# A recurrent turn in which the second gate product, the second convolution's taps and the low parts stand elsewhere

## The chip, the cores and the metric

One core of a Trainium2 chip runs the whole program in one launch. The metric is the device time of an execution in microseconds (us). Of an execution the profiler gives the span, from the first to the last instruction. Five engines matter: PE (matrix products), DVE (VectorE), ACT (ScalarE), POOL (GpSimd) and SP, which here only issues transfers. Each engine works its own list of instructions in order; semaphores order them between engines.

## The reference, cut to what matters

A two-layer encoder on 1040 positions of width 1024. The first layer is a bidirectional gated recurrence of width 2048, and the change lies in it alone:

```python
xb, zb = jnp.split(y @ w_in, 2, axis=-1)
xb = dwconv(xb, conv_w) + conv_b                 # 4 taps over time
for d in range(2):                               # two directions
    r, i = sigmoid(gates of xb, blocks of 256)
    log_a = -8 * softplus(-lam[d]) * r
    a = exp(log_a)
    b = sqrt(-expm1(2 * log_a)) * (i * xb)
    h = a[t] * h[t -+ 1] + b[t]                  # linear recurrence over time
o = (outs[0] + outs[1]) * silu(zb)
```

After it come `o @ w_out`, a norm, the second layer (gated DeltaNet) and a last projection and norm. The code of those is the same in both kernels.

## The kernel before, in words

`rg_loop` works the 2048 channels in eight turns n = 0 to 7, one for each gate block of 256 channels, which are two tiles t = 0, 1 of 128 channels by 1040 positions. Every product is made of three passes of 32-bit operands split in a high and a low part (`project`, L617 to L626: high by high, high by low, low by high). The weights come by units of 128 x 1024: X0 and X1 (columns of x), G0 and G1 (gate weights of one direction each), Z0 and Z1 (columns of z). There are two slots for units, so each unit is loaded by SP, split by POOL (L605 makes the high part, L607 the low part; for G0 and G1 the high part is made by ACT, L612), and used by PE; the slot is free for the next split when PE has done.

PE's turn n is X0 and X1 of the next group n + 1, then the eight gate products q = 0 to 7 of group n, then Z0 and Z1 of group n. In the accumulators, banks 0 to 2 hold the products with t = 0 and banks 3 to 5 those with t = 1. So X1 of one turn may start only when the second gate product `z(1)` of the turn before has read Z1 out of banks 3 to 5, and X0 when `z(0)` has read Z0 out of banks 0 to 2:

```python
e.wait_ge(x_out.sem, x_out.at(n, 2 * t + 2))
e.wait_ge(z_out.sem, z_out.at(n, 2 * t - 2))
columns(n, X0 + t, xtile)
```

"Gate product" here means z times its own sigmoid: ACT makes tanh of half z (L822, two pieces of 832 and 208 positions), DVE multiplies (L906, two pieces) and reads the accumulators a last time.

ACT's turn: copies of x to SBUF (L797), the high parts of G0 and G1 (L612), the eight gate tanhs (L859), the first tap of the next group's convolution (L808), four decays (`decay(i)`: tanh L826, exp L829, square L833), the high parts of the convolved x (`high`, L813), the two z tanhs, and the four square roots (L872). Square roots need another activation table than tanh and exp, and a table load stands where the function's kind changes.

DVE's turn: four products of input gate and x (L923), the three remaining taps of the convolution of each tile of the next group (`convolve`, L638, each tap waits for the one before), the four squared terms (`rest(i)`, L900, which free `asq` for ACT's next square), the two z products, four recurrences (`recur(i)`: a product L913 and a scan L918), two sums (L938) and two last products (L942), after which SP stores the two tiles (L683). PE's gates of the next group need both low parts of x (`low`, POOL, L724), which need `high`, which needs the taps.

Of the kernel before, what the change touches and what calls it, by code (L numbers as in the profile page):

```python
# [554 lines left out]
def hold(e, passed):  # L555


    e.sem_inc(passed, 1)
# [73 lines left out]
    yield ps[:, bank + 2, 0:208], row[:, 832:T]  # L632


def conv_taps(e, acc, xpad, weight, sem, n, base):

    for j in (1, 2, 3):
        e.scalar_tensor_tensor(acc, xpad[:, j:j + T], weight(j), acc, ALU.mult, ALU.add) \  # L638
            .then_inc(sem.sem, 1)
        e.wait_ge(sem.sem, sem.at(n, base + j))  # L640


def rg_loop(nc, sb, ps, c, yhi, ylo, room, w_in, gate_w, o_dram):


    with Phase(nc) as s:
        wt = Weights(nc, sb, s, "rg", (1, 1, 2, 2, 1, 1), 2, ahead=2, room=room, come=1)
        xpad, xc = sb(s, "xpad", [P, 2, T + 4]), sb(s, "xc", [P, 2, T])
# [62 lines left out]
        @block.gpsimd  # L711
        def _(e):
            e.memset(xpad[:, :, 0:1], 0.0)
            e.memset(xpad[:, :, T + 1:T + 4], 0.0).then_inc(pad_done.sem, 1)

            def x_unit(n, t):

                e.wait_ge(xtile.sem, xtile.at(n, t + 1))
                wt.split_unit(e, n, X0 + t, tile, t - 1)

            def low(n, t):
                e.wait_ge(xhi_done.sem, xhi_done.at(n, t + 1))
                hold(e, s.passed)
                e.tensor_tensor(xlo[:, t, :], xc[:, t, :], xhi[:, t, :], ALU.subtract) \  # L724
                    .then_inc(xlo_done.sem, 1)

            def turn(n, more, last):
                gone = 2 if last else 0
                for i in range(2):
                    if last:  # L730
                        wt.split_unit(e, n, G0 + i, tile, i - 1, gate_hi, i, gone)
                    else:
                        wt.split_unit(e, n, G0 + i, xtile, 2 + i + 1, gate_hi, i, gone)
                wt.split_unit(e, n, Z0, tile, 4, gone=gone), wt.split_unit(e, n, Z1, tile, 8, gone=gone)
                for t in range(2):
                    if more:
                        x_unit(n + 1, t)
                    if not last:
                        low(n + 1, t)

            x_unit(0, 0), x_unit(0, 1)
            low(0, 0), low(0, 1)
            with e.Fori(0, LAST - 1) as n:
                turn(n, True, False)
            turn(LAST - 1, False, False)
            turn(LAST, False, True)
# [39 lines left out]
        def _(e):  # L786
# [24 lines left out]
            def high(n, t):  # L811
                e.wait_ge(taps.sem, taps.at(n, 3 * t + 3))
                e.activation(xhi[:, t, :], xc[:, t, :], ACT.Copy).then_inc(xhi_done.sem, 1)  # L813

            def turn(n, last):
                gone = 2 if last else 0

                def z(t):
                    e.wait_ge(tile.sem, tile.at(n, 9 + t))
                    e.wait_ge(odone.sem, odone.at(n, 0))  # L820
                    for src, dst in halves(ps, 3 * t, zs[:, t, :]):
                        e.activation(dst, src, ACT.Tanh, scale=0.5).then_inc(z_tanh.sem, 1)  # L822

                def decay(i):
                    d, t = DT[i]
                    e.activation(u[:, d, t, :], a[:, d, t, :], ACT.Tanh, scale=gp(t, 2 + d),  # L826
                                 bias=gp(t, 2 + d)).then_inc(th_done.sem, 1)
                    e.wait_ge(th_done.sem, th_done.at(n, i + 1))
                    e.activation(a[:, d, t, :], a[:, d, t, :], ACT.Exp, scale=gp(t, d),  # L829
                                 bias=gp(t, d)).then_inc(a_done.sem, 1)  # L830
                    e.wait_ge(a_done.sem, a_done.at(n, i + 1))
                    e.wait_ge(u_done.sem, u_done.at(n, i))
                    e.activation(asq[:, :], a[:, d, t, :], ACT.Square).then_inc(asq_done.sem, 1)  # L833

                e.wait_ge(gate_out.sem, gate_out.at(n, 0))
                e.wait_ge(a_done.sem, a_done.at(n, 0))
                col = 0
                for src, k in ((c["rg_half_c"][:, :], 2), (c["rg_neg_half_c"][:, :], 2),
                               (c["rg_half_gateb"][:, :], 4)):
                    e.activation(gpar[:, :, col:col + k], pick(n, src, k), ACT.Copy).then_inc(gpar_done.sem, 1)  # L840
                    col += k
                e.wait_ge(gpar_done.sem, gpar_done.at(n, 3))
                for t in range(2):
                    if last:
                        wt.hi_unit(e, n, G0 + t, tile, t - 1, gate_hi, gone)
                    else:
                        x_copy(n + 1, t)
                        wt.hi_unit(e, n, G0 + t, xtile, 2 + t + 1, gate_hi, gone)
                for q in range(8):
                    d, g, t = 1 - q // 4, q // 2 % 2, q % 2  # L850
                    e.wait_ge(tile.sem, tile.at(n, q + 1))
                    if q == 0:
                        e.wait_ge(scan.sem, scan.at(n, -2))
                    if q == 4:
                        e.wait_ge(scan.sem, scan.at(n, 0))
                        for b in range(2):
                            e.wait_ge(o_out[b].sem, o_out[b].at(n, 0))
                    for src, dst in halves(ps, 3 * t, (a, v)[g][:, d, t, :]):
                        e.activation(dst, src, ACT.Tanh, scale=0.5,  # L859
                                     bias=gp(t, 4 + 2 * d + g)).then_inc(gate_out.sem, 1)  # L860
                if not last:
                    first_taps(n + 1)
                e.wait_ge(gate_out.sem, gate_out.at(n, 16))
                e.wait_ge(osum.sem, osum.at(n, 0))
                decay(0), decay(1)
                if not last:
                    high(n + 1, 0)
                z(0)
                decay(2), decay(3)
                for i, (d, t) in enumerate(DT):  # L870
                    e.wait_ge(u_done.sem, u_done.at(n, i + 1))
                    e.activation(u[:, d, t, :], u[:, d, t, :], ACT.Sqrt).then_inc(s_done.sem, 1)  # L872
                if not last:
                    high(n + 1, 1)
                z(1)

            x_copy(0, 0), x_copy(0, 1)
            first_taps(0)
# [6 lines left out]
        def _(e):  # L885
# [3 lines left out]
                e.tensor_copy(dpar[:, :, :], taps_of[:, 1:4, bass.ds(n * 2, 2)]).then_inc(dpar_done.sem, 1)  # L889
                e.wait_ge(dpar_done.sem, dpar_done.at(n, 1))  # L890

            def convolve(n, t):
                e.wait_ge(tap0.sem, tap0.at(n, t + 1))
                conv_taps(e, xc[:, t, :], xpad[:, t, :], lambda j: dpar[:, j - 1, t:t + 1], taps, n, 3 * t)

            def turn(n, last):
                def rest(i):
                    d, t = DT[i]
                    e.wait_ge(asq_done.sem, asq_done.at(n, i + 1))
                    e.scalar_tensor_tensor(u[:, d, t, :], asq[:, :], 1.0, u[:, d, t, :],  # L900
                                           ALU.add, ALU.mult).then_inc(u_done.sem, 1)

                def z(t):
                    e.wait_ge(z_tanh.sem, z_tanh.at(n, 2 * t + 2))
                    for src, dst in halves(ps, 3 * t, zs[:, t, :]):
                        e.scalar_tensor_tensor(dst, dst, 1.0, src, ALU.add, ALU.mult) \  # L906
                            .then_inc(z_out.sem, 1)

                def recur(i):
                    d, t = DT[i]  # L910
                    e.wait_ge(s_done.sem, s_done.at(n, i + 1))
                    e.wait_ge(v_done.sem, v_done.at(n, i + 1))
                    e.scalar_tensor_tensor(v[:, d, t, :], u[:, d, t, :], 0.5, v[:, d, t, :],  # L913
                                           ALU.mult, ALU.mult).then_inc(b_done.sem, 1)
                    e.wait_ge(b_done.sem, b_done.at(n, i + 1))
                    order = slice(None) if d == 0 else slice(None, None, -1)
                    states = a[:, 0, t, :] if d == 0 else u[:, 1, t, :]
                    e.tensor_tensor_scan(states[:, order], a[:, d, t, order], v[:, d, t, order], 0.0,  # L918
                                         ALU.mult, ALU.add).then_inc(scan.sem, 1)
# [5 lines left out]
                if not last:  # L925
                    taps_in(n + 1)
                    convolve(n + 1, 0)
                rest(0), rest(1)
                z(0)
                rest(2), rest(3)  # L930
                if not last:
                    convolve(n + 1, 1)
                recur(0)
                z(1)
                recur(1), recur(2), recur(3)
                for t in range(2):
                    e.wait_ge(scan.sem, scan.at(n, 3 + t))
                    e.tensor_tensor(a[:, 0, t, :], a[:, 0, t, :], u[:, 1, t, :], ALU.add) \  # L938
# [1239 lines left out]
```

## Time and profile before

| what | value |
|---|---|
| three runs | 2941.55, 2944.51, 2951.95 us, median 2944.51 |
| profiled execution, span | 2949.6 us (the page gives no other time for it) |
| PE busy, over the span | 2623.1 us, 89% |
| DVE, ACT, POOL busy | 1795.9, 1262.2, 1173.1 us |
| the eight turns of `rg_loop`, PE's first product to DVE's last | 61.56 to 700.05 us |
| PE busy from 210.98 to 286.79 us, one turn | 72.39 of 75.81 us |

The page sums over stages with different limits, so it tells little about a turn. A turn is read from the timelines of the four engines in the same stretch, from the waits of PE, and from the busy time and granted clock of PE in windows cut at its unit boundaries. A timeline row gives the start, the duration, engine, line, operation, tiles and, in brackets, the idle time before it and who ended that.

### The profile page before, as it was taken

The numbers are of one execution on the slowest core, as the hardware profiler recorded it, in microseconds if no ns is written. First come the engines' busy times: TensorE is split into PE (matmuls) and PEld (weight loads), VectorE is DVE, ScalarE is ACT, GpSimd is POOL, SyncE is SP. The second block draws the span as 40 slices with busy tenths as digits, with TensorE's granted clock in tenths as the row PEclk, the third lists the DMA queues.
The fourth block names the chain that finished last, engine by engine and source line by source line (L and its number), as shares of the span: only waits on it lengthen the run. The fifth ranks groups of instructions, "written<-read, shape, count | busy, mean of one in ns | idle before, by whom it ended". The sixth has DMA issues, their size and how long they took to land. (4 is left out here: it accounts for less than half of the span.)

```text
span 2949.6 us, 52298 instructions
## 1 busy us (share of the span) xinstructions
PE 2623.1 (89%) x18311; PEld 2530.2 (86%) x18311; DVE 1795.9 (61%) x2718; ACT 1262.2 (43%) x2180; POOL 1173.1 (40%) x1103
## 2 busy tenths in 40 slices
PE   3999999974997599999999799999998999994995
PEld 3999999974995499999999699998998999994994
DVE  5366666666003487888888757766766677764003
ACT  4455555564013244444444434553554545543012
POOL 4333333321220144445555345555545455543220
PEclk7999999997998799999999879999998999997997
DMA  4111111114113235555555362424234243214113
GB/s 147 44 57 57 52 55 57 57 36 159 44 42 120 56 106 144 137 154 142 156 157 155 109 161 48 123 47 109 76 90 110 47 112 93 69 46 166 43 36 115
DMA packets 244798, 275.48 MB, mean 93 GB/s; under 512 B 86907, under 2 KB 210380, under 8 KB 242972
## 3 DMA queue, kind: packets, MB, share of 16 engines
q1 hardware_dynamic: 240028, 256.31, 30.6%
q10 hardware_dynamic: 4608, 17.04, 1.5%
q8 instruction: 98, 1.61, 0.2%
q14 instruction: 64, 0.52, 0.1%
HBM read 185.78 MB, written 87.53 MB: 93 GB/s over the span
## 5 line engine op out<-in xcount | busy, mean ns | idle before, releaser
L623 PE MATMUL ps<-dn_yhi,dn_whi 128*128 128x416 f32 (+1 forms) x1152 | 395.1, 343 | 10.4 <-ACT p_vrow L1512 5.4
L2006 ACT ACTIVATE zz<-ps 104x416 fp32r<-104x416 f32 x560 | 283.7, 516 | 243.1 <-PE ps L1890 241.3
L624 PE MATMUL ps<-dn_ylo,dn_whi 128*128 128x416 f32 (+1 forms) x1152 | 376.2, 327 | 0.0
L625 PE MATMUL ps<-dn_yhi,dn_wlo 128*128 128x416 f32 (+1 forms) x1152 | 375.7, 326 | 0.0
L2098 DVE TENSOR_TENSOR pp<-ps,level_mask 104x416 fp32r<-104x416 f32 x480 | 276.0, 588 | 136.6 <-PE ps L1890 135.2
L623 PE MATMUL ps<-rg_yhi,rg_whi 128*128 128x416 f32 (+1 forms) x768 | 256.8, 334 | 53.3 <-PEq L80 32.7
L1892 PE MATMUL ps<-pp,zz 104*104 104x208 f32 x1440 | 267.9, 296 | 27.6 <-DVE pp L2098 19.1
L624 PE MATMUL ps<-rg_ylo,rg_whi 128*128 128x416 f32 (+1 forms) x768 | 255.7, 333 | 0.0
L625 PE MATMUL ps<-rg_yhi,rg_wlo 128*128 128x416 f32 (+1 forms) x768 | 254.8, 332 | 0.0
L1892 PE MATMUL ps<-zz,pp 104*104 104x208 f32 x1440 | 248.7, 283 | 0.0
L623 PEld LDWEIGHTS ps<-dn_yhi,dn_whi 128*128 128x128 f32 x1152 | 218.7, 190 | 17.4 <-issue 15.6
L1892 PEld LDWEIGHTS ps<-pp,zz 104*104 104x104 f32 x1440 | 187.9, 177 | 48.6 <-issue 27.8
L624 PEld LDWEIGHTS ps<-dn_ylo,dn_whi 128*128 128x128 f32 x1152 | 218.7, 190 | 3.5 <-issue 2.5
L625 PEld LDWEIGHTS ps<-dn_yhi,dn_wlo 128*128 128x128 f32 x1152 | 218.6, 190 | 1.2
L1843 POOL TENSOR_TENSOR uu<-zz,ident 104x416 fp32r<-104x416 f32 x80 | 88.1, 1123 | 300.1 <-ACT zz L2006 300.1
L623 PEld LDWEIGHTS ps<-rg_yhi,rg_whi 128*128 128x128 f32 x768 | 150.0, 195 | 55.9 <-issue 54.6
L1892 PEld LDWEIGHTS ps<-zz,pp 104*104 104x104 f32 x1440 | 180.1, 178 | 0.0
L623 PE MATMUL ps<-rgo_ohi,rgo_whi 128*128 128x416 f32 (+1 forms) x384 | 126.7, 330 | 43.8 <-POOL rgo_wlo L607 39.7
L607 POOL TENSOR_TENSOR rg_wlo<-rg_raw,rg_whi 128x1024 fp32r<-128x1024 f32 x46 | 118.4, 2574 | 113.7 <-ACT rg_whi L612 111.3
L605 POOL CAST dn_whi<-dn_raw 128x1024 fp32r<-128x1024 f32 x46 | 63.3, 1377 | 249.4 <-issue 168.2
L623 PE MATMUL ps<-dno_ohi,dno_whi 128*128 128x416 f32 (+1 forms) x384 | 126.6, 330 | 38.2 <-POOL dno_wlo L607 34.1
L923 DVE SCALAR_TENSOR_TENSOR v<-v,xc 128x1040 f32<-128x1040 f32 x32 | 72.6, 2272 | 138.0 <-ACT v L859 138.0
(299 smaller groups left out, 7323.6 us busy)
## 6 DMA issues: line engine op xcount, KB each, us to landing
c_nq<-nq_scratch SPq DMA_DIRECT2D x160, 169.0 KB
dn_raw<-in_dn_w_in SPq DMA_DIRECT2D x48, 512.0 KB, 4.2
qd<-rows_scratch SPq DMA_DIRECT2D x160, 104.0 KB, 3.2
rg_raw<-in_rg_w_in SPq DMA_DIRECT2D x32, 512.0 KB, 4.2
nq_scratch<-p_nq SPq DMA_DIRECT2D x48, 338.0 KB
p_ex<-rows_scratch SPq DMA_DIRECT2D x32, 422.5 KB
nq_scratch<-p_rn SPq DMA_DIRECT2D x32, 338.0 KB
o_scratch<-a SPq DMA_DIRECT2D x16, 520.0 KB, 2.8
```

Of the source, the lines that this page charges most:

```text
L605: e.tensor_copy(self.hi[:, slot, :], self.raw[:, slot, :]).then_inc(self.hi_done.sem, 1)
L607: e.tensor_tensor(self.lo[:, slot, :], self.raw[:, slot, :], self.hi[:, slot, :], ALU.subtract) \
L623: e.matmul(o, whi, mhi[:, t0:t0 + tn], start=(first and k == 0), stop=False)
L624: e.matmul(o, whi, mlo[:, t0:t0 + tn], start=False, stop=False)
L625: ins = e.matmul(o, wlo, mhi[:, t0:t0 + tn], start=False, stop=(last and k == end))
L923: e.scalar_tensor_tensor(v[:, d, t, :], v[:, d, t, :], 1.0, xc[:, t, :], ALU.add, ALU.mult).then_inc(v_done.sem, 1)
L1843: e.tensor_tensor(uu[:, b, :, :], zz[:, b, :, :].bitcast(F32), eye, ALU.add) \
L1892: return e.matmul(o, lhs, rhs.unsqueeze(1).to_broadcast([CH, 2, CH]), start=True, stop=True)
L2006: e.activation(zz[:, b, :, :], ps[0:CH, 2 * b + 1, 0:m4], ACT.Copy).then_inc(zev.sem, 1)
L2098: e.tensor_tensor(D4(pp[:, b, l % 2, :, :]), D4(Y4), c["level_mask"][:, l, :, 0:CH].unsqueeze(2).to_broadcast([CH, 2, 2, CH]), ALU.mult).t ...
```

## The change

Three moves in the turn of `rg_loop`, and none in what is computed. On DVE `z(1)` goes from behind the first recurrence to ahead of all four, and the second convolution's three taps, which stood together behind the squared terms, are dealt out: two behind the first squared term, the third behind `z(0)`. On ACT `high(n + 1, 1)` goes from behind the roots to between decays 2 and 3, and `z(1)` from behind the roots to ahead of them. On POOL both low parts go ahead of the split of the next X1.

```diff
-def conv_taps(e, acc, xpad, weight, sem, n, base):
+def conv_taps(e, acc, xpad, weight, sem, n, base, these=(1, 2, 3)):
-    for j in (1, 2, 3):
+    for j in these:
@@ POOL, turn
-                for t in range(2):
-                    if more:
-                        x_unit(n + 1, t)
-                    if not last:
-                        low(n + 1, t)
+                if more:
+                    x_unit(n + 1, 0)
+                if not last:
+                    low(n + 1, 0), low(n + 1, 1)
+                if more:
+                    x_unit(n + 1, 1)
@@ ACT, turn
                 z(0)
-                decay(2), decay(3)
+                decay(2)
+                if not last:
+                    high(n + 1, 1)
+                decay(3)
+                z(1)
                 for i, (d, t) in enumerate(DT):
                     e.wait_ge(u_done.sem, u_done.at(n, i + 1))
                     e.activation(u[:, d, t, :], u[:, d, t, :], ACT.Sqrt).then_inc(s_done.sem, 1)
-                if not last:
-                    high(n + 1, 1)
-                z(1)
@@ DVE, turn
-                rest(0), rest(1)
+                rest(0)
+                if not last:
+                    convolve(n + 1, 1, (1, 2))
+                rest(1)
                 z(0)
+                if not last:
+                    convolve(n + 1, 1, (3,))
                 rest(2), rest(3)
-                if not last:
-                    convolve(n + 1, 1)
-                recur(0)
                 z(1)
-                recur(1), recur(2), recur(3)
+                recur(0), recur(1), recur(2), recur(3)
```

On DVE, in the loop's turn before the change, from the first squared term (u<-asq) through both z products (zs) and the second convolution's taps (xc) to the second recurrence's product (v<-u) the instructions stand so:

```order
L900 SCALAR_TENSOR_TENSOR u<-asq,u 128x1040
L900 SCALAR_TENSOR_TENSOR u<-asq,u 128x1040
L906 SCALAR_TENSOR_TENSOR zs<-zs,ps 128x832
L900 SCALAR_TENSOR_TENSOR u<-asq,u 128x1040
L900 SCALAR_TENSOR_TENSOR u<-asq,u 128x1040
L638 SCALAR_TENSOR_TENSOR xc<-xpad,dpar,xc 128x1040
L638 SCALAR_TENSOR_TENSOR xc<-xpad,dpar,xc 128x1040
L638 SCALAR_TENSOR_TENSOR xc<-xpad,dpar,xc 128x1040
L913 SCALAR_TENSOR_TENSOR v<-u,v 128x1040
L918 SCALAR_TENSOR_TENSOR u<-a,v 128x1040
L906 SCALAR_TENSOR_TENSOR zs<-zs,ps 128x832
```

The same stretch of DVE with the change, where L900 has become L903, L906 L909 and L913 L916:

```order
L903 SCALAR_TENSOR_TENSOR u<-asq,u 128x1040
L638 SCALAR_TENSOR_TENSOR xc<-xpad,dpar,xc 128x1040
L638 SCALAR_TENSOR_TENSOR xc<-xpad,dpar,xc 128x1040
L903 SCALAR_TENSOR_TENSOR u<-asq,u 128x1040
L909 SCALAR_TENSOR_TENSOR zs<-zs,ps 128x832
L638 SCALAR_TENSOR_TENSOR xc<-xpad,dpar,xc 128x1040
L903 SCALAR_TENSOR_TENSOR u<-asq,u 128x1040
L903 SCALAR_TENSOR_TENSOR u<-asq,u 128x1040
L909 SCALAR_TENSOR_TENSOR zs<-zs,ps 128x832
L916 SCALAR_TENSOR_TENSOR v<-u,v 128x1040
L921 SCALAR_TENSOR_TENSOR u<-a,v 128x1040
```

The second z product has passed the three taps, a product and a scan; two taps have come between the first two squared terms, ahead of the first z product.

On ACT, in the loop's turn before the change, from decay 2 (tanh u<-a, exp a<-a, square asq<-a) to the second z tanh the instructions stand so:

```order
L826 ACTIVATE u<-a,gpar 128x1040
L829 ACTIVATE a<-a,gpar 128x1040
L833 ACTIVATE asq<-a 128x1040
L826 ACTIVATE u<-a,gpar 128x1040
L829 ACTIVATE a<-a,gpar 128x1040
L833 ACTIVATE asq<-a 128x1040
L872 ACT_TABLE_LOAD
L872 ACTIVATE u<-u 128x1040 x4
L813 ACTIVATE xhi<-xc 128x1040
L822 ACT_TABLE_LOAD
L822 ACTIVATE zs<-ps 128x832
```

The same stretch of ACT with the change, to the end of the loop's body:

```order
L827 ACTIVATE u<-a,gpar 128x1040
L830 ACTIVATE a<-a,gpar 128x1040
L834 ACTIVATE asq<-a 128x1040
L814 ACTIVATE xhi<-xc 128x1040
L827 ACTIVATE u<-a,gpar 128x1040
L830 ACTIVATE a<-a,gpar 128x1040
L834 ACTIVATE asq<-a 128x1040
L823 ACTIVATE zs<-ps 128x832
L877 ACT_TABLE_LOAD
L877 ACTIVATE u<-u 128x1040 x4
```

The body now ends with the roots; the table load that stood ahead of the second z tanh stands at the head of the body, ahead of the copies to `gpar` (L841), and in turn 7 ahead of the first gate tanh (L860).

## Rows read from the trace of the kernel before

**Rows 1.** Windows, first and last of six turns: stretch, length, busy (instructions) of PE, PEld, DVE, ACT, POOL; granted clock, DMA.

```profile
134.20:210.98 76.78, 73.34 (x435) 72.50 (x433) 50.44 (x31) 41.76 (x53) 26.06 (x12) 0.96 0.18 55
...
515.26:591.04 75.78, 72.35 (x435) 71.58 (x433) 50.53 (x31) 41.76 (x53) 26.40 (x12) 0.98 0.18 56
```

**Rows 2.** PE's waits, 130 to 592 us: us in total, times, longest.

```profile
PE ps L623 <- DVE zs L906: 20.6, 6, 3.4
```

**Rows 3.** Windows of PE alone: stretch, length, busy (instructions), granted clock, DMA.

```profile
210.98:246.37 35.39, 35.39 (x218) 1.00 0.15 44
...
249.79:263.21 13.42, 13.41 (x73) 0.87 0.00 0
263.21:286.79 23.58, 23.58 (x147) 1.00 0.36 112
...
655.80:679.47 23.67, 23.67 (x146) 1.00 0.00 1
```

**Rows 4.** Timeline of DVE, 221 to 250 us.

```profile
221.95 1.24 DVE L900 SCALAR_TENSOR_TENSOR u<-asq,u 128x1040 f32<-128x1040 f32 x1 [0.71 <-ACT asq L833]
225.50 2.18 DVE L900 SCALAR_TENSOR_TENSOR u<-asq,u 128x1040 f32<-128x1040 f32 x1 [2.31 <-ACT asq L833]
227.60 1.29 DVE L906 SCALAR_TENSOR_TENSOR zs<-zs,ps 128x832 f32<-128x832 f32 x2
...
235.68 6.79 DVE L638 SCALAR_TENSOR_TENSOR xc<-xpad,dpar,xc 128x1040 f32<-128x1040 f32 x3
242.50 1.24 DVE L913 SCALAR_TENSOR_TENSOR v<-u,v 128x1040 f32<-128x1040 f32 x1
243.78 4.59 DVE L918 TENSOR_TENSOR_SCAN u<-a,v 128x1040 f32<-128x1040 f32 x1
248.29 1.27 DVE L906 SCALAR_TENSOR_TENSOR zs<-zs,ps 128x832 f32<-128x832 f32 x2
```

**Rows 5.** Timeline of ACT, 226 to 246 us.

```profile
226.32 1.08 ACT L822 ACTIVATE zs<-ps 128x832 f32<-128x832 f32 x2
...
233.42 1.07 ACT L833 ACTIVATE asq<-a 128x1040 f32<-128x1040 f32 x1
234.50 1.28 ACT L872 ACT_TABLE_LOAD   x1
235.80 3.96 ACT L872 ACTIVATE u<-u 128x1040 f32<-128x1040 f32 x4
...
244.88 1.10 ACT L822 ACTIVATE zs<-ps 128x832 f32<-128x832 f32 x2
```

**Rows 6.** Timeline of POOL, 223 to 240 us.

```profile
223.05 1.04 POOL L605 CAST rg_whi<-rg_raw 128x1024 fp32r<-128x1024 f32 x1 [8.22 <-PE ps L625]
224.17 2.41 POOL L607 TENSOR_TENSOR rg_wlo<-rg_raw,rg_whi 128x1024 fp32r<-128x1024 f32 x1
226.60 3.40 POOL L724 TENSOR_TENSOR xlo<-xc,xhi 128x1040 fp32r<-128x1040 f32 x1
234.80 1.86 POOL L605 CAST rg_whi<-rg_raw 128x1024 fp32r<-128x1024 f32 x1 [4.81 <-PE ps L625]
236.74 3.29 POOL L607 TENSOR_TENSOR rg_wlo<-rg_raw,rg_whi 128x1024 fp32r<-128x1024 f32 x1
```

**Rows 7.** Timeline of DVE, 619 to 701 us: ends of turns 6 and 7.

```profile
619.73 1.24 DVE L913 SCALAR_TENSOR_TENSOR v<-u,v 128x1040 f32<-128x1040 f32 x1
...
642.37 2.38 DVE L942 SCALAR_TENSOR_TENSOR a<-a,zs 128x1040 f32<-128x1040 f32 x2
...
678.36 1.24 DVE L913 SCALAR_TENSOR_TENSOR v<-u,v 128x1040 f32<-128x1040 f32 x1 [1.14 <-ACT u L872]
...
683.65 1.30 DVE L906 SCALAR_TENSOR_TENSOR zs<-zs,ps 128x832 f32<-128x832 f32 x2 [1.69 <-ACT zs L822]
...
697.64 2.38 DVE L942 SCALAR_TENSOR_TENSOR a<-a,zs 128x1040 f32<-128x1040 f32 x2
```

**Rows 8.** Timeline of ACT, turn 7: the fifth gate tanh.

```profile
648.50 2.45 ACT L859 ACTIVATE a<-ps,gpar 128x832 f32<-128x832 f32 x4 [5.24 <-DMA o_scratch<-a]
```

More of the change, by code:

```diff
@@ L890, in taps_in, with convolve @@
                 e.wait_ge(dpar_done.sem, dpar_done.at(n, 1))
-            def convolve(n, t):
-                e.wait_ge(tap0.sem, tap0.at(n, t + 1))
-                conv_taps(e, xc[:, t, :], xpad[:, t, :], lambda j: dpar[:, j - 1, t:t + 1], taps, n, 3 * t)
+            def convolve(n, t, these=(1, 2, 3)):
+                if these[0] == 1:
+                    e.wait_ge(tap0.sem, tap0.at(n, t + 1))
+                conv_taps(e, xc[:, t, :], xpad[:, t, :], lambda j: dpar[:, j - 1, t:t + 1], taps, n, 3 * t, these)
             def turn(n, last):
```

## The prediction, made before the changed kernel was run

> **What bounds the kernel now.** The change touches only the eight turns of `rg_loop`, so I read that stretch, and first the windows cut where PE begins the second of its Z and X runs [rows 1]. The reader is to see there that PE is busy for 73.34 of 76.78 us in the first of six like turns and 72.35 of 75.78 in the last; DVE has 50.44, ACT 41.76, POOL 26.06. PE is the engine that fills the turn, and what it does not fill is about 3.4 us. The waits of PE say what that is: over six turns there is one kind of wait, for DVE's z product, 6 times, 20.6 us in all, 3.4 at most [rows 2]. Next the windows of PE within a turn [rows 3]: Z0, Z1 and X0 run without a break for 35.39 us at a granted clock of 1.00, then comes the hole, and X1, which has the same number of products as each of the three, takes 13.42 us at a mean of 0.87. So the hole costs twice: its own 3.42 us (246.37 to 249.79), and then a part of X1 at the lower level of 1.2 GHz, since the clock fell after PE had stood still.
>
> Why X1 waits is in the timelines of DVE and ACT. X1 writes into the banks from which DVE must first read Z1, and DVE comes to that at 248.29, done at 249.56 [rows 4]; PE begins 0.2 us later. ACT got to its z tanh only at 244.88, behind the roots that begin at 235.80 and a table load [rows 5], although Z1 was finished at 234.6 (POOL's cast that waits for Z1 begins at 234.80 [rows 6]). DVE's own queue made it later still: three taps, a product and a scan stand ahead.
>
> **The change, part by part.** I write one loop turn anew, from the durations in the rows; X0 begins at 210.98 + 2 x 35.39 / 3 = 234.57 and is through at 246.37.
>
> *Two taps ahead of the second squared term (DVE).* What decides here is POOL. The squared term at 225.50 takes 2.18 us, not 1.24, and ends 1.1 us behind POOL's copy (224.17 + 2.41 = 226.58) [rows 4, 6]; the three taps take 6.79 us around a POOL copy that ends at 240.03, the last two of them 1.22 us each after it [rows 4, 6]. So I let DVE and POOL take turns where both read SBUF, 1.2 us for a released DVE operation. First squared term done at 223.19; the first tap waits for POOL's cast (224.09) and is done at 225.3; POOL's low copy of X0 227.7; second tap 228.9; POOL's low part of tile 0 (2.3 us alone, 226.60 + 3.40 less what it waited for DVE to 227.68) 231.2; second squared term 232.4; first z product (1.29) 233.7. It ended at 228.89 before [rows 4]. PE needs it at 234.57 for X0, so 0.9 us is left. Without any taking of turns the z product would be done at 228.8; this spread is the first unknown, and I take the late end, because three rows show it.
>
> *Third tap, `high`, decay 3, second z (ACT and DVE).* The third tap ends at 234.9, and ACT's `high` (1.07, like a square) at 236.0. ACT does two decays between 227.40 and 234.49 [rows 5], so 3.55 us each: decay 3 ends at 239.55, the z tanh at 240.65. On DVE the last squared term waits for POOL: POOL's second low part goes from 236.1 to 238.5, then the cast of X1 to 239.5 and its low copy. The squared term ends at 240.8, or 243.1 if the low copy gets in first; the second z product (1.27) at 242.1 to 244.4. X1 needs it at 246.4. The wait of 3.42 us is gone in every turn by this reckoning, with 2 us to spare at least.
>
> *Low parts ahead of X1's split (POOL).* X1's low copy ended at 240.03 [rows 6] and ends now at 241.9 to 243.2; needed at 246.4. SP's load of G1, which waits for that split, is issued up to 3 us later; G1 is used some 20 us later, behind X1 and the first four gates. Cost nothing; if X1's weights were late, PE would wait one for one.
>
> *Roots last (ACT).* First root done at 242.9 at 1.28 for the table and 1.0 for a root. The recurrences begin at 242.9 to 244.4 against 242.50 [rows 4], but with no z product between them. The number of table loads is the same; the one at the head of the next body stands ahead of the x copy of tile 0, which PE needs only behind X1.
>
> *What follows sooner.* With X1 at 246.4 the gates come about 5 us sooner. The fifth gate tanh waits until the turn before has stored its two tiles: 3.75 us from the last product (642.37 + 2.38 = 644.75) to that tanh (648.50) [rows 7, 8]. The chain in turn 7 takes 700.02 - 678.36 = 21.66 us, less 1.69 idle, 1.30 for z, 2.4 for two sums and 2.38: 13.9 for four recurrences [rows 7]. From 244.4 on that gives 263.1, with two POOL copies of 2.4 between 267.9, and the tanh may start at 271.7. The fifth gate product ends at 246.4 + 11.8 + 5 x 23.58 / 8 = 272.9. Hidden, by 1.2 us.
>
> *Sum over six turns.* An unbroken turn is 35.39 + 35.39 / 3 + 23.58 = 70.77 us [rows 3], X1 at full clock, as nothing idles ahead of it. Six are 424.6; before they were 591.04 - 134.20 = 456.84 [rows 1]. That is **-32.2 us**. If the clock were not to come back, X1 would stay at 13.42, and the term would be 6 x 1.62 = 9.7 less. I take the full one, since X0, which follows unbroken work, has 1.00.
>
> *The end.* Turn 7 has no X to hide behind. There the second z product stands ahead of the roots, and the last Z is done at 679.47 [rows 3]: tanh 1.10, table 1.28, root 1.0, so the recurrences begin at 682.9 instead of 678.36, but the 2.99 us of z product and idle between them go: +1.5. Against that, turn 7 starts sooner: its fifth gate tanh waits for the stores of turn 6 (5.24 idle [rows 8]), whose chain from 619.73 to 644.75 [rows 7] loses at least its z product, 1.2 us, and at most that and one block by POOL with the table load, 4. I take 2.5, near the middle, as one block of POOL will stay: **-1.0** in all, between +1.5 and -2.5.
>
> Together -33.2 us. The profiled execution would have 2949.6 - 33.2 = 2916.4 us of span; it lies 5 us above the median of the three runs, and against the median 2944.5 the forecast is **2911.3 us**.
>
> For the switch of tables, the rows have the square done at 234.49, the load at 234.50 and the first root at 235.80: 1.3 us in all [rows 5]. The Trainium skill, ScalarE: Activation LUTs, "What ACT_TABLE_LOAD costs", gives about 1283 ns for the load and some 1380 more for a drain. The row agrees with the first and has no room for the second; by the page turn 7's roots would come 1.4 us later and the kernel would take 2912.7.
>
> **The rivals.** *The wait moves to X0.* The 0.9 us ahead of it are small: one more POOL copy of 2.4 us ahead of a tap or of the squared term, and the first z product is done at 236.1, X0 waits 1.5 us in six turns: 9 us back, 2920. For it speaks that POOL's cast and copies of X0 lie exactly there [rows 6]; against it, that all three of POOL's operations of that time are in my reckoning already. The Trainium skill, SBUF — State Buffer, "Who interferes with whom", is the rule that speaks against the taps' new place: a DVE instruction with two SBUF inputs and a GpSimd one that reads SBUF exclude each other for a whole instruction. The 2.18 and 6.79 us agree with it.
>
> *The wait on Z1's banks stays.* Two POOL copies more ahead of the last squared term put the second z product at 249.2, as late as before; with the end's term some 2943. Against it: POOL has only those operations in a turn.
>
> *The stores set the turn.* Were DVE's chain 4 us longer, the fifth gate tanh would come 3 us behind its product and give back about half of the gain or all of it, 2930 to 2944. DVE's 50.44 of 70.8 us speak against it.
>
> *Slower: X1's weights behind the low part.* POOL may not split X1 before the second low part, and that needs the third tap, `high` and so the first z product. From the end of `high` it is 2.4 + 1.0 + 2.4 and a block of 1.2, 7 us, to X1's weights. If `high` ended later than 242.8 instead of 236.0, X1 would start later than 249.79 and the kernel be slower; at 246 PE would wait 6.6 us a turn, 3.2 more than now: +19, 2963. It takes three blocks more on DVE than the rows allow.
>
> **How the numbers follow.** Forecast 0.78; X0 waits 0.12; Z1's wait stays 0.05; stores 0.02; X1's weights 0.03. Each time is that case's own. A measurement can tell about 0.3% from no change, 9 us. Faster by more than that: the first two, 0.90. Within it: 0.07. Slower: 0.03. The range: below, the end's -2.5 instead of -1.0 and run noise of some 5 us, as the lowest run lies 3 under the median: 2904. Above, X1 at the lower clock, 2921, or X0's waits, 2920, with the end's +1.5: 2924. Outside lies about 0.1, and noise.
>
> **What would show it.** In the profile after: no wait of PE for the z product in turns 1 to 6, X1 at 11.8 us and a clock of 1.00, turns of 70.6 to 70.8 us; the first z product done about 5 us later in the turn than now and the second about 6 sooner; the last products 1 us sooner against the end of PE's turn 6. Wrong would be a wait at X0 with the z product as releaser, a wait at X1 for POOL's low copy, or a clock below 1 in a turn without a hole.

## The result, and the profile after

Seven runs of the changed kernel took 2910.79 to 2927.84 us, median 2921.77, beside seven of the kernel before with a median of 2944.51; the ratio is 0.9902 with a 95% interval of 0.9875 to 0.9929. The forecast, 2911.3 of 2944.5 or 0.9887, lies in that interval, and the median in the range 2904 to 2924, near its upper end. A second set of seven runs gave 2916.78 against a median of 2949.71 over 17 runs of the kernel before, ratio 0.9892 (0.9868 to 0.9917). The profiled execution took 2910.79 us with a span of 2909.1.

The turns first. Windows of the changed kernel, columns as in [rows 1]: the first and the last of six turns, and what is behind them to DVE's last product.

```profile
133.70:204.26 70.56, 70.56 (x434) 70.06 (x433) 50.87 (x31) 41.76 (x53) 27.65 (x12) 1.00 0.20 60
486.50:557.06 70.56, 70.56 (x434) 70.06 (x433) 50.62 (x31) 41.76 (x53) 28.56 (x12) 1.00 0.19 60
557.06:664.65 107.59, 73.83 (x434) 72.65 (x432) 74.96 (x52) 62.05 (x72) 22.15 (x10) 0.85 0.08 26
```

A turn is 70.56 us instead of 75.78 or 76.78 [rows 1], PE is busy in all of it and the clock is 1.00. The list of PE's waits between 130 and 560 us, which held six waits of 3.4 us [rows 2], is empty. Windows of PE alone, X1 of one turn and then Z0 and Z1 of turn 7, as in [rows 3]:

```profile
310.10:321.80 11.70, 11.70 (x74) 1.00 0.00 0
...
618.78:642.44 23.66, 23.66 (x146) 1.00 0.00 1
```

X1 went from 13.42 us at 0.87 to 11.70 at 1.00, right behind X0. The order on DVE around the same place, where PE's timeline has X0 from 298.31 and X1 from 310.06 (DVE's timeline; [rows 4] before):

```profile
285.80 1.24 DVE L903 SCALAR_TENSOR_TENSOR u<-asq,u 128x1040 f32<-128x1040 f32 x1 [0.72 <-ACT asq L834]
286.96 5.44 DVE L638 SCALAR_TENSOR_TENSOR xc<-xpad,dpar,xc 128x1040 f32<-128x1040 f32 x2
292.53 3.26 DVE L903 SCALAR_TENSOR_TENSOR u<-asq,u 128x1040 f32<-128x1040 f32 x1
295.71 1.29 DVE L909 SCALAR_TENSOR_TENSOR zs<-zs,ps 128x832 f32<-128x832 f32 x2
296.93 1.29 DVE L638 SCALAR_TENSOR_TENSOR xc<-xpad,dpar,xc 128x1040 f32<-128x1040 f32 x1
298.34 1.24 DVE L903 SCALAR_TENSOR_TENSOR u<-asq,u 128x1040 f32<-128x1040 f32 x1
302.91 1.24 DVE L903 SCALAR_TENSOR_TENSOR u<-asq,u 128x1040 f32<-128x1040 f32 x1 [3.33 <-ACT asq L834]
304.07 1.30 DVE L909 SCALAR_TENSOR_TENSOR zs<-zs,ps 128x832 f32<-128x832 f32 x2
306.27 1.25 DVE L916 SCALAR_TENSOR_TENSOR v<-u,v 128x1040 f32<-128x1040 f32 x1 [0.91 <-ACT u L877]
```

The first z product is through at 297.00, 1.3 us ahead of X0, and so in each of the six turns; before, it was through 5.6 us ahead (228.89, X0 from 234.47). The second is through at 305.37, 4.7 us ahead of X1; before, 3.2 us late. On ACT (its timeline; [rows 5] before) the second z tanh now follows the last square, and the table load and the roots come after it:

```profile
295.88 1.08 ACT L834 ACTIVATE asq<-a 128x1040 f32<-128x1040 f32 x1 [2.19 <-DVE u L903]
298.25 1.08 ACT L814 ACTIVATE xhi<-xc 128x1040 fp32r<-128x1040 f32 x1 [1.29 <-DVE xc L638]
...
302.78 1.08 ACT L823 ACTIVATE zs<-ps 128x832 f32<-128x832 f32 x2
303.87 1.28 ACT L877 ACT_TABLE_LOAD   x1
305.16 3.96 ACT L877 ACTIVATE u<-u 128x1040 f32<-128x1040 f32 x4
```

Two waits are new on ACT, 2.19 us for the second squared term and 1.29 us for the third tap. Nobody on PE waits for them. POOL in the same stretch (timeline; [rows 6] before):

```profile
286.90 1.04 POOL L605 CAST rg_whi<-rg_raw 128x1024 fp32r<-128x1024 f32 x1 [8.22 <-PE ps L625]
288.02 3.28 POOL L607 TENSOR_TENSOR rg_wlo<-rg_raw,rg_whi 128x1024 fp32r<-128x1024 f32 x1
291.26 3.43 POOL L724 TENSOR_TENSOR xlo<-xc,xhi 128x1040 fp32r<-128x1040 f32 x1
299.50 2.44 POOL L724 TENSOR_TENSOR xlo<-xc,xhi 128x1040 fp32r<-128x1040 f32 x1 [4.81 <-ACT xhi L814]
301.88 1.05 POOL L605 CAST rg_whi<-rg_raw 128x1024 fp32r<-128x1024 f32 x1
303.01 3.40 POOL L607 TENSOR_TENSOR rg_wlo<-rg_raw,rg_whi 128x1024 fp32r<-128x1024 f32 x1
```

X1's low copy ends at 306.41, 3.7 us ahead of X1. The end of the stage on DVE (timeline; [rows 7] before):

```profile
605.35 2.39 DVE L947 SCALAR_TENSOR_TENSOR a<-a,zs 128x1040 f32<-128x1040 f32 x2
...
645.99 1.24 DVE L916 SCALAR_TENSOR_TENSOR v<-u,v 128x1040 f32<-128x1040 f32 x1 [1.08 <-ACT u L877]
...
662.26 2.38 DVE L947 SCALAR_TENSOR_TENSOR a<-a,zs 128x1040 f32<-128x1040 f32 x2
```

And the fifth gate tanh of turn 7 (ACT's timeline; [rows 8] before):

```profile
611.47 2.45 ACT L860 ACTIVATE a<-ps,gpar 128x832 f32<-128x832 f32 x4 [3.56 <-DMA o_scratch<-a]
```

A profile catches one execution of each kernel. For the comparison of kernels I use two lengths from each trace: the **stage**, from PE's first product on `rg_yhi` to the end of DVE's last product (L942 or what it became), and the **chunks**, from PE's first to its last product on `zz`, a later stage in which both kernels have the same code.

| kernel | stage, us | chunks, us | span, us |
|---|---|---|---|
| before | 638.5 | 941.2 | 2949.6 |
| before, again | 637.0 | 942.4 | 2951.2 |
| changed | 603.4 | 934.4 | 2909.1 |
| changed, again | 603.2 | 930.1 | 2903.8 |
| second z product alone | 609.8 | 929.9 | 2908.7 |
| taps, high and low parts alone | 623.9 | 930.0 | 2923.2 |
| first z product later | 612.1 | 930.7 | 2913.7 |
| POOL's order put back | 603.4 | 948.8 | 2925.6 |
| roots first in turn 7 | 600.8 | 939.1 | 2909.5 |
| and stores from z's tile | 598.6 | 946.2 | 2919.0 |

### The profile page after: what moved, and what is told of

Read it like the earlier page. It is cut to its first block and busy times, and to the rows that moved or that the text cites. A ratio compares the mean times of both kernels' runs of the same rounds, so it can differ in the third digit from the quotient of the medians.

```text
span 2909.1 us, 52298 instructions
## 1 busy us (share of the span) xinstructions
PE 2609.5 (90%) x18311; PEld 2517.7 (87%) x18311; DVE 1791.8 (62%) x2718; ACT 1261.8 (43%) x2180; POOL 1183.6 (41%) x1103
## 5 line engine op out<-in xcount | busy, mean ns | idle before, releaser
L623 PE MATMUL ps<-rg_yhi,rg_whi 128*128 128x416 f32 (+1 forms) x768 | 250.7, 326 | 32.0 <-PEq L80 32.0
L607 POOL TENSOR_TENSOR rg_wlo<-rg_raw,rg_whi 128x1024 fp32r<-128x1024 f32 x46 | 131.4, 2857 | 107.8 <-ACT rg_whi L612 105.4
L623 PEld LDWEIGHTS ps<-rg_yhi,rg_whi 128*128 128x128 f32 x768 | 146.1, 190 | 33.4 <-issue 32.2
L624 PEld LDWEIGHTS ps<-rg_ylo,rg_whi 128*128 128x128 f32 x768 | 145.8, 190 | 0.6
```

The lines of the kernel that those rows point to most:

```text
L607: e.tensor_tensor(self.lo[:, slot, :], self.raw[:, slot, :], self.hi[:, slot, :], ALU.subtract) \
L623: e.matmul(o, whi, mhi[:, t0:t0 + tn], start=(first and k == 0), stop=False)
L624: e.matmul(o, whi, mlo[:, t0:t0 + tn], start=False, stop=False)
```

## The experiments

### The changed kernel again, and the kernel before again

No edit in either. For the changed kernel:

> The changed kernel once more, to see which of its times varies. My theory: the gain is in the eight turns alone, from PE's first product to DVE's last of the stage 603 us against 638 before, and that number is the same within 1 us in every profile; what moves the whole time by up to 17 us between executions lies in later stages that the change does not touch, above all the stage of the chunks (941 us in the profile before, 934 after). Rival: the change lets the turns themselves vary, because the first gate product is only about 1 us ahead of X0; then the turns' length differs between profiles by 5 us or more and PE shows waits for the z product.

For the kernel before:

> The kernel before once more, for a second profile of the stages that the change does not touch. Theory: the eight turns take 638 us within 1 us, with six waits of 3.4 us; the stage of the chunks is anywhere between 930 and 945 us. Rival: the stage of the chunks is 941 us again within 1 us, and then the shorter one after the change is the change's doing.

The stage came out at 603.2 and 637.0 us: it repeats within 0.2 us for the changed kernel and within 1.5 for the one before, so my "within 1 us" was a little tight there, and six waits of 3.4 us (20.7 in all) were there again. What varies is the chunks, 930 to 949 us over the ten profiles. Two windows of PE over the whole chunks stage, first of the changed kernel run again, then of the one with POOL's order put back (whose stage is the same 603 us):

```profile
1667.22:2597.29 930.07, 898.79 (x8100) 0.97 0.34 87
```

```profile
1667.79:2616.59 948.80, 911.08 (x8100) 0.96 0.34 86
```

The same 8100 products were busy for 12.3 us more at a lower granted clock, and PE idled 6.4 us more. The rival, that the shorter chunks are the change's doing, is not settled by the second profile of the kernel before: its 942.4 lies only 1.2 us from the first. Against the rival speaks that kernels with all or nearly all of the change in `rg_loop` show 930, 934, 939, 946 and 949, on both sides of those two, and that the medians of the whole times moved by 22.7 and 32.9 us in the two sets, which is not more than the stage's 34 to 35. Why a given execution gets the longer chunks was not tried.

### The second z product alone

```diff
@@ ACT, turn (of the kernel before)
                 decay(2), decay(3)
+                z(1)
                 for i, (d, t) in enumerate(DT):
...
                 if not last:
                     high(n + 1, 1)
-                z(1)
@@ DVE, turn
                 rest(2), rest(3)
+                z(1)
                 if not last:
                     convolve(n + 1, 1)
                 recur(0)
-                z(1)
```

> The kernel before with the second gate product alone moved: on ACT ahead of the roots, on DVE ahead of the second convolution's taps and the recurrences; taps, high part and low parts stay where they were. Theory A, that X1 waited for the second gate product's place in the two queues and for nothing else: no wait of PE in turns 1 to 6, X1 at a clock of 1.00, turns of 70.6 us, the stage 33 to 36 us shorter than before (602 to 606 us). Theory B, that the taps, dealt out among the squared terms, are needed for it: the second gate product still comes too late, PE waits 1 to 3 us a turn and the stage is 5 to 20 us shorter.

No wait of PE between 130 and 560 us. DVE's timeline has the second z product right behind the last squared term, and the taps behind it:

```profile
300.13 1.30 DVE L906 SCALAR_TENSOR_TENSOR zs<-zs,ps 128x832 f32<-128x832 f32 x2
301.35 5.94 DVE L638 SCALAR_TENSOR_TENSOR xc<-xpad,dpar,xc 128x1040 f32<-128x1040 f32 x3
```

The last of its six turns and what lies behind them, columns as in [rows 1]:

```profile
487.00:557.55 70.55, 70.55 (x434) 70.05 (x433) 50.55 (x31) 41.91 (x53) 26.25 (x12) 1.00 0.19 60
557.55:671.12 113.57, 74.42 (x434) 73.07 (x432) 76.76 (x52) 62.19 (x72) 22.76 (x10) 0.85 0.08 25
```

Theory A holds for the six turns: this one move takes the holes away, and the six together are as short (423.35 us) as with the whole change (423.36). The other moves are not needed for that; they use up what the first z product has to spare ahead of X0, which is 5.6 us here and 1.3 with the whole change. But the stage is 609.8 us, 27 to 29 less than before and not the 33 to 36 expected. Of the 6.5 us that it lacks against the change, 6.0 lie behind the six turns (113.57 against 107.59) and 0.5 ahead of them. Behind them the taps stand between z and the recurrences, and the timeline of ACT in turn 7 shows what comes later there:

```profile
601.13 1.28 ACT L859 ACT_TABLE_LOAD   x1 [10.13 <-DVE u L918]
...
616.38 2.45 ACT L859 ACTIVATE a<-ps,gpar 128x832 f32<-128x832 f32 x4 [5.17 <-DMA o_scratch<-a]
```

The first gate tanh of turn 7 waits for the second scan of turn 6 for 10.13 us (4.01 with the whole change), and the fifth, which waits for the stores, comes at 616.38 instead of 611.47. By time the two kernels can't be told apart: ratio 0.9884 (0.9857 to 0.9912) here, 0.9892 (0.9868 to 0.9917) with the whole change.

### The taps, the high and the low parts alone

```diff
@@ ACT, turn (of the changed kernel)
                 decay(3)
-                z(1)
                 for i, (d, t) in enumerate(DT):
                     e.wait_ge(u_done.sem, u_done.at(n, i + 1))
                     e.activation(u[:, d, t, :], u[:, d, t, :], ACT.Sqrt).then_inc(s_done.sem, 1)
+                z(1)
@@ DVE, turn
-                z(1)
-                recur(0), recur(1), recur(2), recur(3)
+                recur(0)
+                z(1)
+                recur(1), recur(2), recur(3)
```

> The changed kernel with the second gate product put back behind the roots on ACT and behind the first recurrence on DVE; the taps are dealt out, the high part is early and the low parts go first, as in the change. Theory A: the hole ahead of X1 stays in part, for high no longer stands between roots and z but decay 3 comes later: 1.5 to 3.5 us a turn with the z product as releaser, and the stage is at most 15 us shorter than before. Theory B: most of the hole goes with these moves, under 1 us a turn, and the stage is 25 us shorter or more.

The ratio is 0.9954 (0.9934 to 0.9975), the stage 13.1 to 14.6 us shorter than before. Its list of PE's waits, 130 to 560 us:

```profile
PE ps L623 <- ACT xpad L798: 11.5, 6, 1.9
```

As theory A had it, a hole of 1.9 us stays, though not under the name of the z product. The releaser named is not the one: in the code X1 waits for no x copy of that time. DVE's timeline shows the z product through at 245.85:

```profile
244.55 1.30 DVE L909 SCALAR_TENSOR_TENSOR zs<-zs,ps 128x832 f32<-128x832 f32 x2 [0.70 <-ACT zs L823]
```

and PE's has X1 at 246.09, 0.24 us behind it, as it was 0.23 behind it before; the x copy, from 245.01 on, only lay beside it in time.

```profile
246.09 0.45 PE L623 MATMUL ps<-rg_yhi,rg_whi 128*128 128x416 f32 x1 [1.91 <-ACT xpad L798]
```

### The first z product later

```diff
@@ DVE, turn (of the changed kernel)
                 rest(1)
-                z(0)
                 if not last:
                     convolve(n + 1, 1, (3,))
-                rest(2), rest(3)
+                rest(2)
+                z(0)
+                rest(3)
```

> The changed kernel with the first gate product put off on DVE, behind the third tap and the third squared term, some 2.5 us later in the turn. In the profile of the changed kernel it ended 1.3 us ahead of X0. Theory, that X0 now has 1.3 us to spare and not more: PE waits for the z product about 1.3 us ahead of X0 in six turns, 8 us in all, and the stage is 8 us longer than 603 us if the clock holds through so short a hole, up to 18 us if it falls as behind the holes of 3.4 us. Rival, that X0's banks are no limit (another wait lets X0 begin late anyway): no wait, the stage stays 603 us.

PE's waits, 130 to 566 us:

```profile
PE ps L623 <- DVE zs L909: 7.6, 6, 1.3
```

The wait is at X0 now, six times, and the stage is 8.7 to 8.9 us longer than in the two profiles of the changed kernel. Two windows of PE, one hole and the X0 and X1 behind it:

```profile
156.91:158.17 1.26, 0.00 (x1) 1.00 0.00 0
...
158.17:181.76 23.59, 23.59 (x145) 1.00 0.08 23
```

The clock held, behind this hole and the five others. So the rival of the prediction, that the wait moves to X0, names a real limit; the change stays 1.3 us on the good side of it.

### POOL's order put back

```diff
@@ POOL, turn (of the changed kernel)
-                if more:
-                    x_unit(n + 1, 0)
-                if not last:
-                    low(n + 1, 0), low(n + 1, 1)
-                if more:
-                    x_unit(n + 1, 1)
+                for t in range(2):
+                    if more:
+                        x_unit(n + 1, t)
+                    if not last:
+                        low(n + 1, t)
```

> The changed kernel with POOL's order put back: X1's split ahead of the second low part. Theory: the order of the low parts changes nothing in the time, since X1's weights are ready 4 us before they are needed and the low part is used behind X1: no wait of PE in turns 1 to 6, the stage 603 us within 1 us. Rival, that the low parts' order is what lets PE run on: holes of 1 us or more a turn, the stage 609 us or more.

No wait of PE in the six turns, stage 603.4 us: the order of the low parts changes nothing. The one run took 2927.4 us, 16.6 more than the profiled run of the changed kernel, and 14.4 of these are its longer chunks (948.8 us, shown above). So of what the second z product alone lacks behind the six turns, the taps and the high part bring all; which of these two does it was not tried apart.

### Roots first in turn 7

```diff
@@ ACT, turn (of the changed kernel)
                 decay(3)
-                z(1)
+                if not last:
+                    z(1)
                 for i, (d, t) in enumerate(DT):
                     e.wait_ge(u_done.sem, u_done.at(n, i + 1))
                     e.activation(u[:, d, t, :], u[:, d, t, :], ACT.Sqrt).then_inc(s_done.sem, 1)
+                if last:
+                    z(1)
@@ DVE, turn
-                z(1)
+                if not last:
+                    z(1)
                 recur(0), recur(1), recur(2), recur(3)
+                if last:
+                    z(1)
```

> The changed kernel with turn 7 alone in another order: there the roots stand ahead of the second gate product on ACT, and all four recurrences on DVE. Theory, that in the last turn the second gate product ahead of the roots costs time, since nothing is left for PE to do behind it: DVE's last product ends 19 us behind PE's last product of the stage instead of 22, the stage is 600 us, 3 less. Rival: the end is set by something else (the stores, or DVE's contention with POOL) and stays 603 us.

Its DVE timeline at the end:

```profile
642.23 1.24 DVE L919 SCALAR_TENSOR_TENSOR v<-u,v 128x1040 f32<-128x1040 f32 x1 [1.14 <-ACT u L878]
...
659.72 2.38 DVE L953 SCALAR_TENSOR_TENSOR a<-a,zs 128x1040 f32<-128x1040 f32 x2
```

The recurrences begin 3.8 us earlier than with the change (645.99), the last product ends 18.8 us behind PE's last instead of 22.2. From PE's begin of Z in turn 6 to the last product it is 104.2 us instead of 107.6. The stage is 600.8 us, only 2.6 less than with the change, because what stands ahead of the six turns, which the edit does not touch, took 0.8 us longer in this execution.

### Stores from z's tile, Z's loads ahead of them

```diff
@@ SP, store and turn (of the kernel with roots first in turn 7)
-                                a[:, 0, t:t + 1, :]).then_inc(o_out[t].sem, 16)
+                                zs[:, t:t + 1, :]).then_inc(o_out[t].sem, 16)
...
+                columns(n, Z0, n * 256 + W, gone), columns(n, Z1, n * 256 + W + P, gone)
                 if not first:
                     store(n)
-                columns(n, Z0, n * 256 + W, gone), columns(n, Z1, n * 256 + W + P, gone)
@@ ACT, z(t), then the fifth gate tanh
-                    e.wait_ge(odone.sem, odone.at(n, 0))
+                    e.wait_ge(o_out[t].sem, o_out[t].at(n, 0))
...
-                        e.wait_ge(scan.sem, scan.at(n, 0))
-                        for b in range(2):
-                            e.wait_ge(o_out[b].sem, o_out[b].at(n, 0))
+                        e.wait_ge(odone.sem, odone.at(n, 0))
@@ DVE, last products
-                    e.scalar_tensor_tensor(a[:, 0, t, :], a[:, 0, t, :], 0.5, zs[:, t, :],
+                    e.scalar_tensor_tensor(zs[:, t, :], a[:, 0, t, :], 0.5, zs[:, t, :],
```

> The kernel of the run before (roots first in turn 7) and two moves more: the last products go to the tile of z and are stored from there, so that the fifth gate tanh waits for DVE's last product and not for the store; and SP loads Z0 and Z1 ahead of the stores. Theory: in turn 7 the wait of 3.6 us for the store goes, Z0's weights come sooner, and the stage is 597 to 599 us, 40 us shorter than before, with no wait in turns 1 to 6. Rival: the fifth gate tanh then waits for another thing of the same length, and the stage is 600 us.

ACT's timeline, the fifth gate tanh of turn 7:

```profile
609.15 1.28 ACT L858 ACTIVATE a<-ps,gpar 128x832 f32<-128x832 f32 x2 [2.08 <-DVE zs L951]
```

It comes at 609.15 instead of 611.47 with the change and waits 2.08 us for the last product and no longer for the store. PE has no wait in the six turns. The stage is 598.6 us, 38 to 40 less than before, 4.7 less than the change and 2.2 less than the run before it; which of the two moves brings that was not tried apart. The ratio is 0.9855 (0.9826 to 0.9884), six runs, median 2908.85 against 2951.72. It is the lowest median here, but its interval overlaps that of the change, and the difference from the change is shown by the stage alone.

## Why the prediction was right, point by point

*The bound.* PE, with one hole a turn whose releaser is the second z product: right, and shown by the move of that product alone, which empties the list and by itself shortens the six turns as much as the whole change does.

*The price of the hole.* The six turns lie from 133.70 to 557.06, 423.36 us, against 456.84: -33.5, where the sum had -32.2. The term was 1.3 us small because each of the four units was counted as a third of 35.39, and that window runs to the end of its last product, which in unbroken work overlaps the next one: the measured turn is 70.56, not 70.77, and X0 began before at 234.47, not 234.57. That X1 would be at full clock was right; the holes alone are 20.6 us, and nearly all of the rest is X1's, which before took 13.3 to 14.6 us in these six turns.

*Two taps among the squared terms.* I had the first z product 0.9 us ahead of X0, by letting DVE and POOL take turns; it is 1.3 ahead, and the instruction times of 5.44 and 3.26 us show the turns taken. Putting it off showed that this margin is real: 1.26 us of wait for some 2.5 us of delay.

*Third tap, high, decay 3, second z.* High done 1.4 us behind X0's begin by the sum, 1.0 measured; second z product 7.5 to 9.8, measured 7.1; X1's low copy 7.3 to 8.6, measured 8.1. The last squared term got in ahead of the low copy, the better of the two cases, and it did not wait for POOL, as I had it: it began at 302.91, right behind ACT's square (302.88), and took its plain 1.24 us.

*Low parts ahead of X1's split.* Costs nothing, as said, and brings nothing: 603.4 us with either order. The slower rival has its condition far away: X1's weights are 3.7 us early.

*The stores.* The last product of a turn was to be done at most 33.3 us behind X0's begin. In the turn shown it is done at 329.30 (324.71 + 4.59 on DVE), 31.0 behind, and PE shows no wait in any of the six turns.

*The end.* From PE's begin of Z in turn 6 to the last product it is 107.59 us instead of 109.01: -1.4, forecast -1.0. Both halves were there: the chain behind PE's last product is 22.2 us instead of 20.6 (+1.6, forecast +1.5), and PE's part is 85.4 instead of 88.4 (-3.0, forecast -2.5). That the second z product ahead of the roots costs something in the last turn is shown by the run that puts the roots first there.

*The switch of tables.* The last square ends at 302.88, the second z tanh at 303.86, the load begins at 303.87 and the first root at 305.16: the whole switch is again 1.3 us, without the further 1380 ns that the Trainium skill, ScalarE: Activation LUTs, "What ACT_TABLE_LOAD costs", names for a drain.

*The total.* The stage gave -34 to -35, the sum -33.2. The profiled execution, forecast at a span of 2916.4 us, has 2909.1: 35.1 less in the stage and, what the sum had at nothing, 6.8 less in the chunks. The first set's median lies 10 us above the forecast nonetheless. The base is not the reason: the seven runs of the kernel before in that set have the same median, 2944.51, that the forecast was taken from, so the medians differ by 22.7 us there, against 32.9 in the second set. The run noise of some 5 us was too small a term, since the runs of the kernel before in the first set lie from 2940.49 to 2967.04 and the chunks alone differ by up to 19 us between executions. What made those seven runs long is not shown, as only the first of them was profiled; two of them, 2927.73 and 2927.84, lie above the range. That the mechanism was right is read from the traces; that the first median fell inside the range was in part luck.

## What to carry to other kernels

When the busiest engine has one hole a turn, look in the queue of the engine that ends it: here a product of 1.3 us, ready early, stood behind roots, taps and a scan, and moving it alone gave all of the gain in the six turns and some 28 of the 35 us of the stage. Count what the hole costs behind it as well, here more than half as much again, and say what the moved work puts at risk, to the microsecond; the 1.3 us ahead of X0 were found so. The last turn has other limits than those before it and wants an order of its own.

## What the runs showed of the hardware that I had not expected

After two holes of the same length the clock of X1 was not the same. In the kernel with taps, high and low parts alone, these are two windows of PE over X1 behind holes of 1.91 us:

```profile
171.79:185.21 13.42, 13.42 (x73) 0.87 0.00 0
246.09:257.93 11.84, 11.84 (x73) 1.00 0.00 0
```

In one the granted clock fell to the lower level for a part, in the other not, with the same work before and after; of that kernel's six holes four were followed by a fall. Behind the hole of 3.42 us it had fallen [rows 3], behind the six of 1.25 to 1.28 us it stayed. Even a hole as long as those of the kernel before need not cost the clock. This is one in the second profile of that kernel, and the X1 behind it:

```profile
169.07:172.51 3.44, 0.00 (x1) 1.00 0.00 0
172.51:184.36 11.85, 11.85 (x73) 1.00 0.00 0
```

Of the twelve holes of 3.41 to 3.46 us in the two profiles of the kernel before, eleven were followed by a fall and this one was not. So the second cost of a hole that the prediction counts is the rule here, and not certain for each hole.

And the chunks stage, the same code in all ten profiles, was 930 to 949 us long, with a mean granted clock of 0.97 in the shorter of the two windows shown and 0.96 in the longer. That spread is half of what the change brings, so the profile's stage, which repeats within 1.5 us, tells more of such a change than the times do.
